# A two-block transformer kernel on one Trainium2 core: the mLSTM head norm spread over its neighbours, and weight halves and modulation slabs reordered at two norms

## The chip, the cores and the metric

The kernel runs on one core of a Trainium2 chip. The metric is the device time of one execution in microseconds. Three runs of the kernel before took 2473.16, 2465.38 and 2474.76 us; their median is 2473.16 us.

## The reference, cut to what matters

Two blocks are computed for 512 latent and 256 context tokens of width 1024, in fp32. The first ends in a convolutional feed-forward layer between two post-norms. The second starts with a mixer of two halves: an mLSTM (4 heads of 128, both directions over chunks of 128 tokens) and a banded window attention (8 heads of 64). What the change touches:

```python
def post_norm(x, y, gate, g, b):
    return layer_norm(ALPHA * x + gate * y) * g + b

def modulate(x, shift, scale):
    return layer_norm(x) * (1 + scale) + shift          # first block
    # second block: rms_norm(x, g) * (1 + scale) + shift

def mlstm_out(h, oa):                                    # h = forward + backward mLSTM output
    h = rms_norm(h.transpose(0, 2, 1, 3), a_norm_g.reshape(A_HEADS, A_HEAD_DIM))
    return (h.reshape(b, t, A_WIDTH) * sigmoid(oa)).astype(oa.dtype)

y = concatenate([mlstm_out(ha, oa), ob], axis=-1) @ w_out    # ob: the window attention
```

The shifts, scales and gates are six rows of `silu(c) @ w_ada + b` for each block.

## The kernel before, in words

The program is a row of blocks. In each block every engine (TensorE, VectorE, ScalarE, GpSimd, and SyncE for the transfers) has its own list of instructions in a fixed order, and the semaphores are written out by hand; all engines meet at a block's end. Activations lie with channels on the partitions (xT, hT: 8 tiles of 128 channels by 768 tokens), the latent range is 512 columns and the context range 256.

All big weights come as slabs of 1024 x 256 through a ring of four slots. `load_slabs` (L321) issues the load of a slab once the slab four places before has been used. A slab of a projection is split into two exact parts: ScalarE copies a half (128 columns) in rounded form (`high`, L1027 and L2538), GpSimd subtracts (`low`, L1033 and L2586), and TensorE makes three products per tile with the parts of the activations. A slab of the modulation (`ada_slab`, L852) is used straight from the ring by 8 matmuls; it gives its slot back when they are done.

Three places matter.

**The norms ahead of the feed-forward layer (ln1) and ahead of the second mixer (ln2).** At both, a post-norm (`post`) is followed by the modulated norm of the next stage (`norm`). A norm that centres sums its input over the 8 tiles on TensorE (L448), takes the mean on ScalarE (L556), spreads it over the partitions (L456), subtracts it on VectorE (L614), squares on ScalarE (L572), sums the squares (L448), takes the root (ScalarE L536) and the reciprocal (VectorE L605), spreads it (L456), multiplies (VectorE L630), and applies gain and shift on ScalarE (`outs`, L598). A split norm then writes the rounded part (VectorE L640) and the rest (GpSimd L646), tile by tile, and TensorE starts on the projection with the first tile. Two hooks let other work in: `gaps`, run by TensorE at named places, and `fill`, run by ScalarE right after the root. Before, at ln1, the four slabs of the gate modulation stand in the gaps "mean" and "root" of the two norms, and `post.fill` copies three weight halves: two of the first slab of `ffn_w_up`, and one of the second. At ln2, `norm` does not centre, and it is the kind that does its context range first (`ctx_first`): its latent squares are taken on ScalarE (L589) from what VectorE has just scaled, and its sums follow on TensorE after the spread of the context range. There all four modulation slabs stand in one gap, "start", between the post-norm's spread and the norm's, and `post.fill` copies three halves of the first two slabs of `ab_w_in` and the narrow part.

**The mLSTM recurrence (L3495 on).** 12 steps, forward and backward in turn. Per step: TensorE makes the gate rows (L3505), the scores (L3512), the outputs (L3528, L3529) and the state update (L3535); ScalarE takes two exponentials (L3611 "iw", L3613); GpSimd scales queries and keys (L3627, L3628); VectorE masks (L3548, L3556, L3559), takes the denominators (L3572 to L3575), and updates the state (L3590). The first direction to reach a chunk writes its output by ScalarE (L3603), the second adds to it by VectorE (L3580); that second kind is steps 2, 3, 8, 9, 10 and 11. ScalarE ends with four sigmoids (L3618).

**The head norm (L3639 to L3689)** is a block of its own: squares on ScalarE (L3643), their sums on VectorE (L3664), root (L3647), reciprocal (L3666), six multiplications on VectorE (L3668), 24 transposes on TensorE (L3688), and eight copies out with the norm's gain (L3654, L3675). It also turns the key halves of the attention (L3681, L3661).

**The attention's pairs (L3047 on).** 24 pairs of a pair of heads and a token chunk, numbered p. Per pair: scores on TensorE (L3091), masked maximum on VectorE (L3161), exponential on ScalarE (L3201), division on VectorE (L3171, L3173), transposes on TensorE (L3103) and copies out of them (ScalarE L3209, VectorE L3181), values on TensorE (L3117), and their copy out (L3215), which GpSimd splits (L689, L690). Pairs with n = 1, 2 are wide (5 key blocks), those with n = 4, 5 are short (2 blocks). At pairs 0 to 3 GpSimd also multiplies the mLSTM half by the sigmoids and splits it (`gated_side`: L3056, L689, L690 on 128 x 768). Twelve modulation slabs are used at the short pairs (L852). Before pair 0, GpSimd writes the mask bands (L3064 to L3066) and VectorE the negated sinks (L3146).

The order of one pair on TensorE is written out by hand:

```python
for p in range(n_p):
    if p + 2 < n_p:
        scores(p + 2)
    ...
    turn(p)
    if p >= 1:
        values(p - 1)
```

## Time and profile before

| | us |
|---|---|
| three runs | 2465.38, 2473.16, 2474.76 |
| median | 2473.16 |
| profiled execution, its own time | 2473.65 |
| its span, first to last instruction | 2471.8 |
| mean granted TensorE clock, share of full | 0.968 |

The profiled execution is one run of the same program with the hardware profiler on. Its own time is 1.85 us more than its span. Times in the rows count from the first instruction. PE is TensorE's matmuls, PEld its weight loads, DVE VectorE, ACT ScalarE, POOL GpSimd, SP the queue of transfers; "PEq" as a releaser is TensorE's sequencer, which stands here for the end of a block. A matmul's duration contains its run through the array, so the pace of a row of them is read from start to start.

### The profile page before, as it was taken

The page shows a single profiled execution, that of the slowest core. Times are in us where ns is not written, and L with a number is a line of the kernel's source. Part 1 is how long each engine was busy: PE and PEld are TensorE (multiplying, and loading weights), DVE is VectorE, ACT ScalarE, POOL GpSimd, SP SyncE. Part 2 cuts the span into 40 slices and gives each one's busy share as a digit, 9 for nine tenths or more (in the row PEclk, how much of TensorE's full clock was granted, in tenths as well). Part 3 has the DMA queues.
Part 4 walks back from the last instruction along what each step waited for, and adds up shares of the span by engine and source line. Part 5 has one row for each costly group of instructions (what it writes and reads, how often), then busy time and mean ns, then how long its engine had stood idle before and what let it go on. Part 6 is the DMA issues. An engine that isn't in the chain of part 4 may idle for free. (4 is left out here: it accounts for less than half of the span.)

```text
span 2471.8 us, 35014 instructions
## 1 busy us (share of the span) xinstructions
PE 2334.2 (94%) x14351; PEld 1921.0 (78%) x14351; DVE 1151.1 (47%) x1893; ACT 797.6 (32%) x1343; POOL 1052.1 (43%) x715
## 2 busy tenths in 40 slices
PE   6999979999997999969899999999999999999999
PEld 5876747878774789856778888888887788788887
DVE  4647368665635660678345151322347652411111
ACT  4334353333325312335242121111134364322221
POOL 3436345555544122323246343433443024746553
PEclk8999989999997999979999999999999999999999
DMA  8335235444452111005112132321212102223221
GB/s 265 105 102 171 86 103 187 158 140 146 151 166 82 39 52 60 27 1 188 52 35 85 53 103 93 96 95 59 69 43 69 35 1 69 85 87 118 88 86 47
DMA packets 223933, 228.39 MB, mean 92 GB/s; under 512 B 7375, under 2 KB 221347, under 8 KB 223779
## 3 DMA queue, kind: packets, MB, share of 16 engines
q1 hardware_dynamic: 223443, 226.09, 28.4%
q8 instruction: 114, 1.87, 0.3%
q14 instruction: 40, 0.33, 0.0%
q10 hardware_dynamic: 336, 0.11, 0.0%
HBM read 224.08 MB, written 2.10 MB: 92 GB/s over the span
## 5 line engine op out<-in xcount | busy, mean ns | idle before, releaser
L1411 POOL TENSOR_TENSOR w_lo<-ring,w_hi 128x1024 fp32r<-128x1024 f32 x124 | 301.2, 2432 | 315.7 <-ACT w_hi L1405 315.7
L2355 DVE SCALAR_TENSOR_TENSOR xT<-ps,mods,xT 128x512 f32<-128x512 f32 (+1 forms) x160 | 108.4, 683 | 546.3 <-PE ps L1473 510.1
L1405 ACT ACTIVATE w_hi<-ring 128x1024 fp32r<-128x1024 f32 x124 | 130.6, 1057 | 503.4 <-PE ps L1473 503.4
L1471 PE MATMUL ps<-hidden_hi,w_hi 128*128 128x512 f32 (+1 forms) x768 | 272.4, 355 | 0.0
L1472 PE MATMUL ps<-hidden_lo,w_hi 128*128 128x512 f32 (+1 forms) x768 | 272.1, 354 | 0.0
L1473 PE MATMUL ps<-hidden_hi,w_lo 128*128 128x512 f32 (+1 forms) x768 | 271.8, 354 | 0.0
L2644 DVE SCALAR_TENSOR_TENSOR ffn_sums<-ps,cols,ffn_sums 128x441 f32<-128x441 f32 (+2 forms) x352 | 214.9, 686 | 105.8 <-ACT ffn_sums L2563 105.8
L1471 PE MATMUL ps<-h_hi,w_hi 128*128 128x512 f32 (+1 forms) x720 | 255.6, 355 | 3.6 <-POOL w_lo L1411 2.1
L1472 PE MATMUL ps<-h_lo,w_hi 128*128 128x512 f32 (+1 forms) x720 | 255.2, 354 | 0.0
L1473 PE MATMUL ps<-h_hi,w_lo 128*128 128x512 f32 (+1 forms) x720 | 254.8, 354 | 0.0
L2586 POOL TENSOR_TENSOR ffn_w_lo<-ring,ffn_w_hi 128x1024 fp32r<-128x1024 f32 (+2 forms) x76 | 161.7, 2129 | 191.9 <-ACT ffn_w_hi L2538 191.9
L1054 PE MATMUL ps<-h_hi,w_halves 128*128 128x512 f32 (+1 forms) x560 | 205.7, 367 | 11.1 <-POOL ab_lo L646 5.2
L2724 DVE TENSOR_TENSOR squares<-squares 128x512 f32<-128x512 f32 (+1 forms) x72 | 96.5, 1341 | 217.9 <-ACT squares L2710 217.9
L1471 PEld LDWEIGHTS ps<-hidden_hi,w_hi 128*128 128x128 f32 x768 | 145.3, 189 | 21.1 <-issue 0.8
L1033 POOL TENSOR_TENSOR ring_low<-ring,w_halves 128x1024 fp32r<-128x1024 f32 x31 | 77.1, 2494 | 197.2 <-ACT w_halves L1027 197.2
L1473 PEld LDWEIGHTS ps<-hidden_hi,w_lo 128*128 128x128 f32 x768 | 145.2, 189 | 20.3
L1472 PEld LDWEIGHTS ps<-hidden_lo,w_hi 128*128 128x128 f32 x768 | 145.3, 189 | 19.8
L1471 PEld LDWEIGHTS ps<-h_hi,w_hi 128*128 128x128 f32 x720 | 136.2, 189 | 24.4 <-POOL w_lo L1411 2.8
L2538 ACT ACTIVATE ffn_w_hi<-ring 128x1024 fp32r<-128x1024 f32 (+2 forms) x76 | 71.9, 947 | 255.9 <-PE ps L2527 233.7
L1473 PEld LDWEIGHTS ps<-h_hi,w_lo 128*128 128x128 f32 x720 | 136.1, 189 | 19.0
L1472 PEld LDWEIGHTS ps<-h_lo,w_hi 128*128 128x128 f32 x720 | 136.2, 189 | 18.7
L1054 PE MATMUL ps<-h_hi,ring_low 128*128 128x512 f32 (+1 forms) x384 | 134.8, 351 | 0.0
(473 smaller groups left out, 5192.1 us busy)
## 6 DMA issues: line engine op xcount, KB each, us to landing
ring<-in_mlp_w SPq DMA_DIRECT2D x64, 1024.0 KB, 5.3
ring<-in_ada_w SPq DMA_DIRECT2D x48, 1024.0 KB, 5.3
ring<-in_w_ada SPq DMA_DIRECT2D x24, 1024.0 KB, 5.3
ring<-in_ffn_w_up SPq DMA_DIRECT2D x22, 1024.0 KB, 5.3
ring<-in_ab_w_in SPq DMA_DIRECT2D x11, 1024.0 KB, 5.3
ring<-in_ffn_w_down SPq DMA_DIRECT2D x12, 768.0 KB, 4.5
ring<-in_w_in SPq DMA_DIRECT2D x8, 1024.0 KB, 8.6
ring<-in_c_w_in SPq DMA_DIRECT2D x6, 1024.0 KB, 5.0
```

The costliest lines, as they stand in the source:

```text
L1033: pool.tensor_tensor(low_half(h), ring_half(h), w_halves[:, h % 3, :, :].bitcast(F32), ALU.subtract)\
L1054: ins = pe.matmul(o, stationary, moving, start=(k == 0 and i == 0), stop=(k == KT - 1 and i == 2))
L1405: act.activation(w_hi[m][:, 0:x["kt"], :], ring[:, x["n"] % NS, 0:x["kt"], m * P:(m + 1) * P], ACT.Copy).then_inc(SW["w_hi"].sem, 1)
L1411: pool.tensor_tensor(w_lo[m][:, 0:x["kt"], :], ring[:, x["n"] % NS, 0:x["kt"], m * P:(m + 1) * P], w_hi[m][:, 0:x["kt"], :].bitcast(F32), ...
L1471: pe.matmul(o, w_hi[m][:, k, :], h, start=(k == 0), stop=False)
L1472: pe.matmul(o, w_hi[m][:, k, :], l, start=False, stop=False)
L1473: ins = pe.matmul(o, w_lo[m][:, k, :], h, start=False, stop=(k == x["kt"] - 1))
L2355: return nc.vector.scalar_tensor_tensor(x, bank, column_of(gates, t * 2 + 2 * gate + r), x, ALU.mult, ALU.add)
L2538: act.activation(w_hi[i % NW][:, 0:kt, :], ring[:, n % NS, 0:kt, m * P:(m + 1) * P], ACT.Copy).then_inc(SW["w_hi"].sem, 1)
L2586: pool.tensor_tensor(w_lo[i % NW][:, 0:kt, :], ring[:, n % NS, 0:kt, m * P:(m + 1) * P], w_hi[i % NW][:, 0:kt, :].bitcast(F32), ALU.subtract)\
L2644: ins = dve.scalar_tensor_tensor(o, on_grid(ps[:, (first + m) % 4, :])[:, y0 + dy:y1 + dy, x0 + dx:x1 + dx], cols[:, CW + tap * 2 * FT + t ...
L2724: dve.tensor_tensor(sq, sq, sq, ALU.mult).then_inc(v_order.sem, 1)
```

## The change

The head norm's block is dissolved. Its squares and their sums are taken by ScalarE in the recurrence, one chunk at a time once both directions have added to it (steps 2, 3, 8, 9, 10), each as four squares of 128 x 128 with an accumulator; the last chunk's, the root and the reciprocal open the attention's block. GpSimd multiplies (six times 128 x 512) ahead of the pairs. TensorE's 24 transposes come in six lots behind pairs 3, 4, 5, 6, 9 and 10, through one bank, and ScalarE copies them out. The gating of the mLSTM half moves from pairs 0 to 3 to pairs 11 to 14. The turned key halves are made in step 0 of the recurrence, the bands and the sinks in the block of transposes before it. The state update is left out in the last two steps, where nothing reads it. The table for the root is loaded at the end of the recurrence.

At both norms the four modulation slabs now follow the second and the fifth sum of squares of `post` and of `norm`, and `post.fill` copies only the two halves of the first slab; the rest is copied in `norm.fill`.

```diff
@@ -493,6 +493,7 @@
             for k in range(KT):
                 self.wait(pe, "sq", KT + k + 1)
                 self.sig(self.sums(pe, 0, squares[:, k % 3, 0:LAT], 192, LAT // 4, k == 0, k == KT - 1), "sq_used")
+                self.in_gap(pe, k)
...
@@ -502,6 +503,8 @@
                 self.lead.pe(pe, u)
             self.wait(pe, "sq", u + 1)
             self.sig(self.sums(pe, r, squares[:, u % 3, 0:n], 192 + c, w_, k == 0, k == KT - 1), "sq_used")
+            if r == 0:
+                self.in_gap(pe, k)
...
@@ -588,6 +591,8 @@
                     self.next.wait(act, "sq_used", KT + k - 2)
                 self.next.sig(act.activation(squares[:, k % 3, 0:LAT], self.where(k), ACT.Square,
                                              bias=self.shift(k, 0), scale=self.scale(k, 0)), "sq")
+            if self.next.fill is not None:
+                self.next.fill(act)
             self.next.root(act, 0, 2 * KT)
...
-            def late_slabs(pe):
-                for j in range(4):
-                    ada_slab(pe, 1, W["ada_2"] + j, 0, j, j == 3)
+            def late_slab(j):
+                return lambda pe: ada_slab(pe, 1, W["ada_2"] + j, 0, j, j == 3)
...
-                norm.gaps = {"start": late_slabs}
+                post.gaps = {1: late_slab(0), 4: late_slab(1)}
+                norm.gaps = {1: late_slab(2), 4: late_slab(3)}
                 post.pe(pe)
...
-                for h in range(0 if post is not None else 1, min(3, n_halves)):
+                for h in range(2 if post is not None else 1, min(3, n_halves)):
...
+            def first_parts(act):
+                for h in range(2):
+                    high(act, h)
...
-                (norm if post is None else post).fill = rest_of_parts
+                else:
+                    post.fill = first_parts
+                norm.fill = rest_of_parts
...
-        post.gaps = {"mean": gate_slab(0), "root": gate_slab(1)}
-        norm.gaps = {"mean": gate_slab(2), "root": gate_slab(3)}
+        post.gaps = {1: gate_slab(0), 4: gate_slab(1)}
+        norm.gaps = {1: gate_slab(2), 4: gate_slab(3)}
...
+        def first_parts(some):
+            def fill(act):
+                for i in some:
+                    high(i)
+            return fill
+        post.fill, norm.fill = first_parts(range(2)), first_parts(range(2, NW))
...
+                mix.wait_out(pool, mix.needed(i))
                 g_order.step(pool, pool.tensor_tensor(dst, dst, factor, ALU.mult))
                 made.split(pool, i, 0, TOK)
...
-            g_order.step(pool, pool.memset(bands, 0.0))
-            pool.tensor_copy(bands[:, PREV * CH:(PREV + 1) * CH], mats[:, M_PREV, :])
-            sig(pool.tensor_copy(bands[:, NEXT * CH:(NEXT + 1) * CH], mats[:, M_NEXT, :]), "bands")
+            mix.scaled(pool)
             for p in range(n_p):
-                if p < len(side):
-                    gated_side(pool, p)
+                if p in mix.side_at:
+                    gated_side(pool, mix.side_at.index(p))
...
+                    mix.wait_out(pe, mix.turns_until(p))
                     pe.wait_ge(ADA["ada_rows_out"].sem, ADA["ada_rows_out"].at(p // 6))
                 turn(p)
                 if p >= 1:
                     values(p - 1)
+                if p in mix.turn_at:
+                    mix.turn(pe, mix.turn_at.index(p))
...
-            wait(dve, "bands", 1)
-            sig(dve.tensor_scalar(nsink, rows[:, SINK:SINK + B_HEADS], -1.0, None, ALU.mult), "nsink")
-            wait(dve, "nsink", 1)
...
             top(0)
+            mix.inverse(dve)
...
+            mix.roots(act)
             expo(0)
...
                     give(p - 1)
+                if p in mix.turn_at:
+                    mix.out(act, mix.turn_at.index(p))
...
+        dve.tensor_scalar(nsink, rows[:, SINK:SINK + B_HEADS], -1.0, None, ALU.mult)
         transpose_out(dve, groups, 0)
...
+        g_order.step(pool, pool.memset(bands, 0.0))
+        for at, mask in ((2, M_PREV), (4, M_NEXT)):
+            pool.tensor_copy(bands[:, at * CH:(at + 1) * CH], mats[:, mask, :])
...
+n_mem = n_m - 2
+def chunk_squares(act, c):
+    for h in range(4):
+        ins = act.activation(sq_junk[:, h * P:(h + 1) * P], h_tok[:, c, h, :], ACT.Square, accum_out=ssq[:, c, h:h + 1])
+    return ins
...
         front(0)
+        for r, (t0, n) in enumerate(BOTH):
+            ins = pe.matmul(ps[:, 6 + r, 0:n], mats[:, SWAP, :], kb[:, 0, t0:t0 + n], start=True, stop=True)
+        sig(ins, "swapped")
...
+            if s >= n_mem:
+                continue
             wait(pe, "kw", s + 1)
+            if s == 0:
+                wait(pe, "out_v", 1)
...
             if s + 1 < n_m:
                 masked(s + 1)
+            if s >= n_mem:
+                continue
...
+                wait(act, "h", s + 1)
+                chunk_squares(act, c)
...
+                wait(act, "swapped", 1)
+                for r, (t0, n) in enumerate(BOTH):
+                    ins = act.activation(kb[:, 1, t0:t0 + n], ps[:, 6 + r, 0:n], ACT.Copy)
+                sig(ins, "out_v")
             if s >= 1:
                 give(s - 1)
-        give(n_m - 1)
         for t in range(4):
             act.activation(oa[:, t, :], oa[:, t, :], ACT.Sigmoid)
+        act.activation(warm[:, :], eps_col, ACT.Sqrt)
...
-sq_tok = k_tok.rearrange("p c (h e) -> p c h e", h=4)
-ssq = small[:, 0:4 * NCH].rearrange("p (c h) -> p c h", h=4)
-R = named("sq", "ssq", "std", "scaled", "turned", "out_a", "out_v", "swapped")
-out_groups = [(h, c0, n) for h in range(4) for c0, n in ((0, NLAT), (NLAT, NCTX))]
-bank_of = lambda g: (out_groups[g][0], 0) if out_groups[g][1] == 0 else (4 + out_groups[g][0] % 2, 256 * (out_groups[g][0] // 2))
-with nc.Block() as block:
-    @block.scalar
-    def _(act):
-        for j in range(3):
-            sig(act.activation(sq_tok[:, 2 * j:2 * j + 2, :, :].rearrange("p c h e -> p (c h e)"),
-                               h_tok[:, 2 * j:2 * j + 2, :, :].rearrange("p c h e -> p (c h e)"), ACT.Square), "sq")
-        wait(act, "ssq", 3)
...
-        a_order.step(act, act.activation(flat_s, flat_s, ACT.Sqrt, bias=eps_col, scale=1.0 / P))
-        sig(act.activation(flat_s, flat_s, ACT.Copy), "std")
...
-    @block.vector
-    def _(dve):
-        wait(dve, "swapped", 1)
-        for r, (t0, n) in enumerate(BOTH):
-            dve.tensor_copy(kb[:, 1, t0:t0 + n], ps[:, 6 + r, 0:n])
-        for j in range(3):
-            wait(dve, "sq", j + 1)
-            sig(dve.tensor_reduce(ssq[:, 2 * j:2 * j + 2, :], sq_tok[:, 2 * j:2 * j + 2, :, :], AX_X, ALU.add), "ssq")
-        wait(dve, "std", 1)
...
-    @block.tensor
-    def _(pe):
-        for r, (t0, n) in enumerate(BOTH):
-            ins = pe.matmul(ps[:, 6 + r, 0:n], mats[:, SWAP, :], kb[:, 0, t0:t0 + n], start=True, stop=True)
-        sig(ins, "swapped")
-        for c in range(NCH):
-            wait(pe, "scaled", c + 1)
-            for h in range(4):
-                b, o = bank_of(2 * h + int(c >= NLAT))
-                o += (c - (NLAT if c >= NLAT else 0)) * CH
-                ins = pe.transpose(ps[:, b, o:o + CH], h_tok[:, c, h, :], ident)
-        sig(ins, "turned")
-for n, v in (("sq", 3), ("ssq", 3), ("std", 1), ("scaled", NCH), ("turned", 1), ("out_a", 4), ("out_v", 4), ("swapped", 1)):
...
+class MixerNorm:
+    turn_at, side_at = [3, 4, 5, 6, 9, 10], [11, 12, 13, 14]
+    units = [[(h, c) for c in range(NLAT)] for h in range(4)] + \
+            [[(h, NLAT + c) for h in (2 * j, 2 * j + 1) for c in range(NCTX)] for j in range(2)]
+    BANK = 7
+    def __init__(self):
+        self.R = named("ssq", "std", "rd", "scaled", "swapped", "out_a")
+        self.flat = ssq.rearrange("p c h -> p (c h)")
+        self.src = qa.rearrange("p t n -> p (t n)").rearrange("p (c h e) -> p c h e", c=NCH, h=4)
...
+    def needed(self, i):
+        return 5 + i // 2
+    def turns_until(self, p):
+        return sum(at < p for at in self.turn_at)
+    def roots(self, act):
+        self.sig(chunk_squares(act, order_m[-1][1]), "ssq")
+        self.wait(act, "ssq", 1)
+        self.sig(act.activation(self.flat, self.flat, ACT.Sqrt, bias=eps_col, scale=1.0 / P), "std")
+    def inverse(self, dve):
+        self.wait(dve, "std", 1)
+        self.sig(dve.reciprocal(self.flat, self.flat), "rd")
+    def scaled(self, pool):
+        self.wait(pool, "rd", 1)
         for c in range(NCH):
-            sig(dve.tensor_tensor(h_tok[:, c, :, :], h_tok[:, c, :, :],
-                                  ssq[:, c, :].unsqueeze(2).to_broadcast([P, 4, P]), ALU.mult), "scaled")
...
+            self.sig(pool.tensor_tensor(self.src[:, c, :, :], h_tok[:, c, :, :],
+                                        ssq[:, c, :].unsqueeze(2).to_broadcast([P, 4, P]), ALU.mult), "scaled")
+    def turn(self, pe, i):
+        self.wait(pe, "scaled", NCH)
+        if i:
+            self.wait(pe, "out_a", i)
+        for j, (h, c) in enumerate(self.units[i]):
+            ins = pe.transpose(ps[:, self.BANK, j * CH:(j + 1) * CH], self.src[:, c, h, :], ident)
+        self.sig(ins, "swapped")
+    def out(self, act, i):
+        self.wait(act, "swapped", i + 1)
+        runs = [(h, 0, NLAT, 0) for h in [i]] if i < 4 else \
+               [(h, NLAT, NCTX, (h % 2) * CTX) for h in (2 * (i - 4), 2 * (i - 4) + 1)]
+        for h, c0, n, o in runs:
+            ins = act.activation(hT[:, h, c0 * CH:(c0 + n) * CH], ps[:, self.BANK, o:o + n * CH], ACT.Copy,
+                                 scale=cols[:, COL["mlstm_norm"] + h:COL["mlstm_norm"] + h + 1])
+        self.sig(ins, "out_a")
```

## Rows read from the trace of the kernel before

**Rows 1.** The page's first part: busy time of each engine

```profile
PE 2334.2 (94%) x14351; PEld 1921.0 (78%) x14351; DVE 1151.1 (47%) x1893; ACT 797.6 (32%) x1343; POOL 1052.1 (43%) x715
```

**Rows 2.** Windows of the attention: stretch, length, busy by engine, PEclk, DMA share, GB/s

```profile
1093.90:1107.00 13.10, 11.06 (x37) 5.74 (x38) 6.61 (x21) 4.83 (x13) 1.15 (x1) 0.50 0.00 0
1107.00:1199.00 92.00, 85.26 (x865) 57.15 (x864) 72.27 (x218) 48.59 (x136) 36.77 (x59) 0.96 0.43 138
```

**Rows 3.** Timeline, recurrence's end to first pairs: start, duration, engine, instructions, [idle before <-releaser]

```profile
1063.37 1.13 DVE L3580 SCALAR_TENSOR_TENSOR hT<-ps,small,hT 128x128 f32<-128x128 f32 x4
...
1063.37 1.28 ACT L3618 ACT_TABLE_LOAD   x1
1064.66 3.04 ACT L3618 ACTIVATE big<-big 128x768 f32<-128x768 f32 x4
1072.53 2.95 ACT L3643 ACTIVATE big<-hT 128x1024 f32<-128x1024 f32 x3 [4.82 <-PEq L3495]
...
1089.12 1.20 PE L3091 MATMUL ps<-big 64*128 64x256 f32 x8 [2.55 <-PEq L3639]
1093.94 2.94 PE L3091 MATMUL ps<-big 64*128 64x384 f32 x12 [3.62 <-DVE small L3161]
...
1092.33 0.15 DVE L3160 COPY big<-small 128x1 f32<-128x1 f32 x1
```

**Rows 4.** Timeline of two recurrence steps: ScalarE and VectorE

```profile
1025.90 0.60 ACT L3611 ACTIVATE hT<-ps 128x512 f32<-128x512 f32 x1 [1.65 <-PE ps L3505]
...
1048.51 1.14 ACT L3603 ACTIVATE hT<-ps,small 128x128 f32<-128x128 f32 x4 [0.47 <-DVE small L3575]
...
1024.72 1.13 DVE L3580 SCALAR_TENSOR_TENSOR hT<-ps,small,hT 128x128 f32<-128x128 f32 x4
1028.12 1.12 DVE L3548 TENSOR_SCALAR hT<-ps,small 128x128 f32<-128x128 f32 x4
```

**Rows 5.** Timeline of the attention's pairs (L3628: the recurrence): TensorE, VectorE, GpSimd

```profile
1118.55 0.66 PE L3103 MATMUL ps<-mats,big 128*128 128x128 f32 x4
...
1124.62 1.85 DVE L3173 TENSOR_SCALAR big<-big,small 128x512 f32<-128x512 f32 x1
1134.83 0.49 DVE L3173 TENSOR_SCALAR big<-big,small 128x512 f32<-128x512 f32 x1
...
1047.12 1.04 POOL L3628 TENSOR_TENSOR big<-big,small 128x512 f32<-128x512 f32 x1
...
1124.31 1.87 POOL L690 TENSOR_TENSOR h_hi<-hT,ab_out_hi 128x768 fp32r<-128x768 f32 x1
```

**Rows 6.** Timeline of the norms ahead of the feed-forward layer (ln1)

```profile
326.30 1.06 ACT L2538 ACTIVATE ffn_w_hi<-ring 128x1024 fp32r<-128x1024 f32 x1 [5.35 <-DMA ring<-in_ffn_w_up]
327.26 5.74 ACT L598 ACTIVATE xT<-xT,cols 128x512 f32<-128x512 f32 x8
...
328.12 5.59 PE L448 MATMUL ps<-xT,mats 128*32 128x128 f32 x64 [6.86 <-ACT xT L598]
336.11 1.94 PE L852 MATMUL ps<-ring,sil 128*32 128x256 f32 x16
```

**Rows 7.** Timeline of the norms ahead of the second mixer (ln2)

```profile
759.01 2.00 ACT L1027 ACTIVATE w_halves<-ring 128x1024 fp32r<-128x1024 f32 x2 [10.68 <-DMA ring<-in_ab_w_in]
...
751.48 4.87 DVE L630 TENSOR_TENSOR xT<-xT,ps 128x512 f32<-128x512 f32 x8 [2.17 <-PE ps L456]
...
751.37 5.69 PE L852 MATMUL ps<-ring,sil 128*32 128x256 f32 x64
764.11 1.97 PE L456 MATMUL ps<-rstd,mats 128*128 128x64 f32 x8 [7.04 <-DVE rstd L605]
766.01 5.12 PE L448 MATMUL ps<-squares,mats 128*32 128x128 f32 x64
...
753.43 46.54 SPq L321 DMA_DIRECT2D ring<-in_ab_w_in  x5
```

**Rows 8.** Window within ln1: columns as in the second group

```profile
328.00:339.00 11.00, 10.14 (x108) 4.75 (x112) 2.78 (x5) 7.34 (x13) 1.81 (x1) 0.50 0.00 0
```

52 lines of the change are left out of this document (24 added, 28 removed).

## The prediction

> **What bounds the kernel now.** I read the page first: TensorE is busy 94% of the span [rows 1], so almost everywhere only the matmuls set the time, and a change can gain only where TensorE stands still. Then the windows and the timelines of the three stages that the change touches, engine by engine, and the waits in them.
>
> Head norm. TensorE is nearly always busy in the recurrence and in the pairs (85.26 of 92 us there [rows 2]), but between them lies a serial block: from 1072.53 squares, sums, root, reciprocal, scaling, transposes and copies follow one another, and the attention's first scores start at 1089.12. The second scores start only at 1093.94, because they wait for VectorE's first maxima, and these wait for bands and sinks written at the block's start [rows 3].
>
> ln1. ScalarE stands 5.35 us before the third weight half until its slab lands, and behind it stands L598; TensorE waits 6.86 us for L598's first tile and then follows it tile by tile for 5.59 us [rows 6]. The clock granted there is 0.50, the lower of its two levels (1.2 GHz) [rows 8].
>
> ln2. TensorE runs all four slabs after the post-norm's spread; the first projection slab can only then be issued (753.43), and ScalarE waits 10.68 us for it in `post.fill` [rows 7]. Behind that stand the context's root, its spread (764.11), and the latent sums (766.01 to 771.13), on which the rest of the norm hangs.
>
> **The sum, part by part.** It is made against the profiled execution's own 2473.65 us (span 2471.8 and 1.85 around it), which is 0.5 above the median of the runs shown.
>
> A1, the block goes. VectorE's addition of step 10 ends at 1064.50 [rows 3]. ScalarE then has four squares with accumulators. No row shows a square of that shape. Below: four copies of 128 x 128 take 1.14 us in L3603 [rows 4]. Above: four pieces of 0.60, the time of a whole 512-column exponential, 2.4 us. I take 1.75, nearer the copies, with a little for each accumulator's read. Then the sigmoids' table and the sigmoids as now (1.28 and 3.04), and the root's table, priced as the other, 1.28 with 0.2 for its dummy root: 1064.5 + 1.75 + 4.33 + 1.5 = 1072.1. VectorE's last addition ends before that, its last state update (about 1.1 us) being gone. The meeting of the engines costs about 0.3, so with A2's 0.6 the attention's block opens at 1073.0. First scores 1.20, first maxima 1093.94 - 1092.33 = 1.6 [rows 3], and the second scores start at about 1075.9 instead of 1093.94: **-18.0**. Beside this, ScalarE takes the last chunk's squares (1.75), root (0.3) and the exponential's table (1.28), ready at 1076.4, hidden by the first scores and maxima but for half a us, which the next exponential absorbs; the reciprocal stands behind the first maxima on VectorE. GpSimd's six multiplications, at 1.04 each as L3628 [rows 5], end near 1082.5, long before TensorE wants them behind pair 3.
>
> A2, squares in the recurrence. After steps 2, 3, 8 and 9 they stand on ScalarE ahead of the next step's first exponential. VectorE's addition ends at 1025.85, it wants that exponential's result at 1028.12, and the exponential takes 0.60 [rows 4]: 1.67 us are free, and 1.75 are needed. Behind the delayed exponential GpSimd's query scaling waits, which TensorE wants 3 us later. Four steps by 0.1 to 0.2: **+0.6**, counted above; 0 to 3 by the ends of the square's price. The turning of the keys in step 0 (two matmuls, two copies of some 1.0 us) meets a TensorE that waits for VectorE anyway: 0, at most 0.5. The bands and sinks move to a block whose copies outlast them: 0.
>
> A3, what TensorE gets back in the pairs. Twenty-four transposes in six lots of four; four take 0.66 with the tail, about 0.59 from start to start [rows 5]: 6 x 0.59 = **+3.5**, on the path, since TensorE is the bound there. ScalarE's copies (4.3 us in all) lie in its idle time, and the one bank is free again a pair later. Ends: +3 and +6, if the lots also make it wait.
>
> A4, GpSimd's gating later. Four times L3056, L689, L690, some 4.5 us each by L690's 1.87 [rows 5] and its neighbours, now at pairs 11 to 14, three of which have no modulation slab to lengthen TensorE's part. What the row shows: L3173 takes 0.49 alone and 1.85 while GpSimd runs [rows 5]. At pairs 0 to 3 this cost TensorE nothing visible, so 0 is the lower end; above, half of GpSimd's 18 us beyond VectorE's slack, some 5 us. I take **+1.5**, near the row. The queue of transfers is not moved past anything here. A in all: -18.0 + 3.5 + 1.5 = **-13.0**; -16 to -7.
>
> The Trainium skill, page "GPSIMD Engine Reference", section "Specifications", says that GpSimd shares its SBUF interfaces with VectorE and contends with instructions in a two-port mode or with two SBUF inputs. By that rule every L3173 beside the moved work is held, and the trace agrees (1.85 against 0.49).
>
> B1, ln1. The first gate slab now ends behind the second sum of squares, near 315.9, 2.3 us later than now; its successor's load needs about 5 us, so ScalarE gets its halves at 321.0, copies two (2.0) and starts L598 at 323.0 instead of 327.26: **-4.3**. The third half is copied after the next root, in idle time. The price: two slabs now stand between the norm's sums instead of in gaps with free time. At full clock they fit between squares that come every 0.6 us: 0.3. At half clock each takes 1.94 [rows 6] and the sums run late by up to 3.4. The wait before L598's first tile shrinks from 6.9 us to about 2.5, so the clock may stay up. I take +1.8, the middle, as the rows show no wait of 2.5 here: B1 = **-2.5**; -5.5 (full clock, a faster spread too) to +0.5.
>
> B2, ln2. The first slab ends near 745.2; issue to use took 5.6 us (753.43 to 759.01), so the halves are copied from 750.9 to 752.9. The context's root follows, but its reciprocal stands on VectorE behind L630, which ends at 756.35 [rows 7]: that is what is late next. Reciprocal to 757.0, spread 1.97, sums 5.12 [rows 7] and two slabs of 1.94: 768.0 at half clock, against 771.1 now, -3.1. All at full clock, with the fill ahead of the root: 763.5, -7.6. Before, the clock granted rose while the four slabs ran densely; here the dense work begins only at 757, so I take half of the stretch as fast: B2 = **-4.5**, ends -8 and -1. Loads of later slabs are issued some 9 us later, 20 us before they are needed.
>
> Sum: 2473.65 - 13.0 - 2.5 - 4.5 = **2453.6 us**, 0.8% below before.
>
> **The rivals.** First, only the head norm pays: the slabs between the sums run at half clock and eat what the earlier L598 and halves give. For: 0.50 in both stretches [rows 8]. Against: at ln2 even half clock leaves 3 us. 2473.65 - 13 + 0 = 2460.6.
>
> Second, the clock stays up: shorter waits keep TensorE at 2.4 GHz through both norms. -5.5 - 8 - 15 gives 2445. For: through the post-norms, with matmuls for a third of the time, it was full. Against: it was low behind each of these long waits [rows 8].
>
> Third, VectorE becomes the pairs' bound: the 18 us of gating hold L3173 wherever they meet it. With nearly all of them on the path (+13) A is about -3, and with B 2463. For: [rows 5]; against: pairs 1 to 4 bore the same work and TensorE hardly idled.
>
> Fourth, slower. The removed block held 24 transposes in a row; without them the clock, low from the recurrence's end until 1107 now [rows 2], rises later. Pairs at half clock take twice TensorE's time; each us of full-clock work so done costs one. From 20 us of such work, five pairs, the gain is gone; with eight pairs, some 30 us, it is 2484. Against: scores two onward keep TensorE dense, as before.
>
> That the change doesn't do what it says I give nothing: each hook has its caller in the diff.
>
> **How the numbers follow.** Forecast 0.6, only the head norm 0.15, clock up 0.12, VectorE 0.09, slower 0.04. A measurement of this kernel tells about 0.5%, 12 us, from no change, i.e. 2461. The forecast's own bounds, not all at once, give 2445 to 2461; to this come the rivals on either side and the runs' own 4 us: 2442 to 2464 leaves out the slow case and the fastest part of the second. Faster by over 0.5%: the forecast, the clock case and the first rival, 0.87, less 0.03 for the runs' scatter about the last, which lies near the bound: 0.84. Within: 0.12. Slower: 0.04.
>
> **What would show it.** Right: second scores of the attention about 18 us earlier against the recurrence's start; TensorE gapless through pairs 3 to 10 and longer by 3.5; L598 in ln1 starting with two halves and no third ahead of it; in ln2 the reciprocal of the context right behind L630, and the latent root 3 to 5 us earlier. Wrong: L3611 late by over 0.5 us per step, TensorE idle at pairs 11 to 14, PEclk of 0.5 past the attention's second pair, or ScalarE waiting for a slab in either norm for longer than 3 us.

## The result and the profile after

The changed kernel takes 2440.64 us (median of 4 runs, 2438.72 to 2442.74), the kernel before in the same measurement 2471.5 (2465.38 to 2474.76): ratio 0.9881, 95% interval 0.9865 to 0.9896. Measured once more beside 17 runs of before (e6, below) the ratio is 0.9905, interval 0.9890 to 0.9920. So it is faster by some 1 to 1.2%, 23 to 29 us, where 20 were forecast. The sign and the kind were right; 2440.64 itself lies 1.4 below the range's lower end.

Lines of the norms stand 5 lower in the changed kernel (L598 is L603, L852 is L857), scores L3091 are L3103, the scaling L3173 is L3184.

First part of the page of the changed kernel [rows 1], then two windows of it, its columns as in [rows 2]: the first pairs and the rest of them.

```profile
PE 2314.1 (95%) x14335; PEld 1909.8 (78%) x14335; DVE 1143.0 (47%) x1870; ACT 805.5 (33%) x1394; POOL 1060.4 (43%) x719
```

```profile
1062.78:1074.90 12.12, 10.12 (x34) 5.45 (x36) 6.77 (x21) 5.39 (x13) 6.21 (x6) 0.50 0.00 0
1074.90:1171.00 96.10, 87.88 (x894) 58.64 (x890) 73.64 (x220) 53.43 (x146) 41.68 (x62) 0.98 0.41 132
```

The stretch at half clock behind the second scores has stayed (12.1 us against 13.1), so the slower rival is out. TensorE's work per pair has grown.

To see where the time went I took the starts of the same TensorE instructions in each trace and cut the span there. Differences of starts, in us; the last two columns are all the rest of the span, and the span. The cuts, with their starts before and after: the context's last transposes ahead of ln1 (308.03, 306.70), a product at the end of the feed-forward layer (735.96, 732.20), the first product of the second mixer's projection (779.86, 769.35), the recurrence's first step (1007.66, 995.70), the attention's second scores (1093.94, 1062.78), the tiles of L861 (1189.31, 1162.65), the first product of the output projection (1199.18, 1171.11).

| profile | ln1 and feed-forward | ln2 | recurrence to second scores | pairs to L861 | their end | the rest | span |
|---|---|---|---|---|---|---|---|
| before | 427.94 | 43.89 | 86.28 | 95.37 | 9.87 | 1808.5 | 2471.8 |
| before again (e5) | 428.13 | 43.73 | 86.55 | 95.31 | 9.75 | 1808.1 | 2471.6 |
| after | 425.50 | 37.15 | 67.08 | 99.87 | 8.46 | 1800.8 | 2438.8 |
| after again (e6) | 425.54 | 37.15 | 67.08 | 99.87 | 8.45 | 1801.4 | 2439.5 |
| e1, head norm only | 428.13 | 43.76 | 67.09 | 101.02 | 9.82 | 1804.8 | 2454.6 |
| e2, ln1 only | 425.60 | 43.44 | 84.26 | 95.13 | 9.65 | 1805.1 | 2463.2 |
| e3, ln2 only | 428.00 | 37.14 | 86.54 | 95.16 | 9.80 | 1807.2 | 2463.8 |
| e4, weights early | 425.76 | 37.15 | 67.07 | 99.73 | 6.86 | 1801.7 | 2438.2 |
| e7, without ln1 | 427.56 | 37.18 | 68.02 | 100.78 | 9.69 | 1805.9 | 2449.1 |
| e8, without ln2 | 425.68 | 41.56 | 67.09 | 99.88 | 10.12 | 1804.0 | 2448.3 |
| e9, few transposes | 425.63 | 37.15 | 67.09 | 97.90 | 9.70 | 1809.7 | 2447.1 |
| e10, gating in slab pairs | 425.77 | 37.15 | 67.07 | 99.89 | 8.46 | 1800.8 | 2439.1 |
| e11, squares twice | 425.65 | 37.14 | 72.54 | 100.24 | 9.29 | 1803.1 | 2448.0 |
| e12, gating and weights | 425.62 | 37.15 | 67.22 | 97.16 | 6.85 | 1805.0 | 2439.0 |

Between the first profiles the edited stages give -2.4, -6.7, -19.2, +4.5 and -1.4, in all -25.3. The rest of the span gives another 7.7, without an edit in it. Over the fourteen profiles that rest is anything from 1800.8 to 1809.7, and I can tie its value to no edit (the changed kernel, 1800.8, and e9, 1809.7, do the same work there). Part of it may be low clock, of which the whole span has less after (by the mean clock, 0.968 before and 0.976 after, (1 - 0.968) x 2471.8 / 0.5 = 158 us before against 117). The mean clock alone doesn't give it either: e9 and e11 have the same, 0.972, and rests of 1809.7 and 1803.1. A single pair of profiles is thus no measure of the total. A stage is a better one, but not an exact one: where e2 has the old mixer its recurrence to second scores lasts 84.26 and not 86.3 to 86.5, where e8 has the old ln2 that lasts 41.56 and not 43.4 to 43.9, and the same pairs take 99.87 in the change and 101.02 in e1.

**The opening.** Timeline of the changed kernel, from the last recurrence step to the second pair [rows 3]:

```profile
1053.87 1.28 ACT L3663 ACT_TABLE_LOAD   x1
1055.16 3.04 ACT L3663 ACTIVATE big<-big 128x768 f32<-128x768 f32 x4
1057.98 1.13 DVE L3617 SCALAR_TENSOR_TENSOR hT<-ps,small,hT 128x128 f32<-128x128 f32 x4
1058.21 1.28 ACT L3664 ACT_TABLE_LOAD   x1
1060.00 1.14 PE L3103 MATMUL ps<-big 64*128 64x256 f32 x8 [2.66 <-PEq L3525]
1062.64 0.30 DVE L3718 RECIPROCAL small<-small 128x24 f32<-128x24 f32 x1
1062.78 2.94 PE L3103 MATMUL ps<-big 64*128 64x384 f32 x12 [1.64 <-DVE small L3172]
1063.02 6.21 POOL L3723 TENSOR_TENSOR big<-hT,small 128x512 f32<-128x512 f32 x6 [12.52 <-DVE small L3718]
```

The serial block of squares, sums, root, scaling and transposes is gone. The first scores come 2.0 behind the start of the last addition, the reciprocal stands on VectorE behind the first maxima and holds nothing back, and GpSimd scales beside the pairs. What sets the opening now is ScalarE's row of sigmoids and two tables.

**The squares in a step** (timeline of a recurrence step, ScalarE and VectorE, [rows 4]):

```profile
1042.19 0.31 ACT L3521 ACTIVATE squares<-hT 128x128 f32<-128x128 f32 x1 [1.63 <-DVE hT L3617]
...
1043.28 0.19 ACT L3521 ACTIVATION_READ_ACCUMULATOR squares<-hT 128x1 f32 x1
1043.37 0.57 ACT L3652 ACTIVATE hT<-ps 128x512 f32<-128x512 f32 x1
...
1044.43 1.12 DVE L3585 TENSOR_SCALAR hT<-ps,small 128x128 f32<-128x128 f32 x4
```

Four squares with their reads take 1.28 (1042.19 to 1043.47), and VectorE takes the exponential's result 0.5 behind its end. All steps keep their length: against before, the first step's values start 11.95 earlier and the last step's 11.94.

**The pairs** (timeline of the changed kernel, [rows 5]): a lot of transposes between the values ahead of it and the scores behind it; an instruction of GpSimd's first gating with the VectorE scaling beside it, and TensorE's three waits; the third gating, which begins just before a modulation slab on TensorE; and the two subtractions of the next weights at pair 19 with the longest wait.

```profile
1083.74 1.31 PE L3129 MATMUL ps<-big 128*64 128x128 f32 x20
1084.98 0.66 PE L3731 MATMUL ps<-mats,big 128*128 128x128 f32 x4
1085.57 1.13 PE L3103 MATMUL ps<-big 64*128 64x256 f32 x8
...
1123.04 1.81 POOL L695 TENSOR_TENSOR h_hi<-hT,ab_out_hi 128x768 fp32r<-128x768 f32 x1
1123.23 1.96 DVE L3184 TENSOR_SCALAR big<-big,small 128x640 f32<-128x640 f32 x1
1125.45 0.74 PE L3115 MATMUL ps<-mats,big 128*128 128x128 f32 x5 [0.51 <-DVE big L3184]
1126.60 0.73 PE L3115 MATMUL ps<-mats,big 128*128 128x128 f32 x5 [0.41 <-DVE big L3192]
1130.36 0.74 PE L3115 MATMUL ps<-mats,big 128*128 128x128 f32 x5 [0.67 <-DVE big L3192]
1131.95 2.00 POOL L3070 TENSOR_TENSOR hT<-hT,big 128x768 f32<-128x768 f32 x1
1132.90 1.07 PE L857 MATMUL ps<-ring,sil 128*32 128x256 f32 x16
...
1157.13 4.71 POOL L689 TENSOR_TENSOR ab_out_w<-ring,ab_out_w 128x1024 fp32r<-128x1024 f32 x2
1157.89 1.76 DVE L3184 TENSOR_SCALAR big<-big,small 128x256 f32<-128x256 f32 x1
1159.76 2.24 DVE L3184 TENSOR_SCALAR big<-big,small 128x256 f32<-128x256 f32 x1
1162.65 1.92 PE L866 MATMUL ps<-mats,mean 128*128 128x32 f32 x12 [3.65 <-DVE big L3192]
```

**ln1** (timeline, [rows 6]): the first gate slab now runs behind the second sum, the load behind it is issued at 314.65, and two halves, not three, stand ahead of L603.

```profile
313.54 1.05 PE L857 MATMUL ps<-ring,sil 128*32 128x256 f32 x16
314.65 2.16 SPq L321 DMA_DIRECT2D ring<-in_ffn_w_up  x2
319.75 2.00 ACT L2549 ACTIVATE ffn_w_hi<-ring 128x1024 fp32r<-128x1024 f32 x2 [2.00 <-DMA ring<-in_ffn_w_up]
321.65 5.74 ACT L603 ACTIVATE xT<-xT,cols 128x512 f32<-128x512 f32 x8
322.51 5.59 PE L448 MATMUL ps<-xT,mats 128*32 128x128 f32 x64 [2.57 <-ACT xT L603]
333.04 1.93 PE L857 MATMUL ps<-ring,sil 128*32 128x256 f32 x16
```

**ln2** (timeline, [rows 7]), and two windows of it with the granted clock (0.50, then 1.00):

```profile
741.52 47.92 SPq L321 DMA_DIRECT2D ring<-in_ab_w_in  x5
746.74 2.00 ACT L1032 ACTIVATE w_halves<-ring 128x1024 fp32r<-128x1024 f32 x2 [2.18 <-DMA ring<-in_ab_w_in]
746.79 4.87 DVE L635 TENSOR_TENSOR xT<-xT,ps 128x512 f32<-128x512 f32 x8 [1.25 <-PE ps L456]
751.58 0.54 DVE L610 RECIPROCAL rstd<-rstd 128x64 f32<-128x64 f32 x1
...
760.70 0.35 ACT L539 ACTIVATE rstd<-ps,mats 128x128 f32<-128x128 f32 x1
```

```profile
747.20:757.40 10.20, 5.22 (x56) 4.08 (x60) 4.92 (x9) 5.37 (x8) 4.67 (x2) 0.50 0.19 60
757.50:764.20 6.70, 3.45 (x61) 2.07 (x52) 1.87 (x3) 6.70 (x11) 2.76 (x2) 1.00 0.97 305
```

ScalarE's 10.68 us for the slab are 2.18 now, and the context's reciprocal starts in the moment in which VectorE's last product L635 ends, as forecast.

### The profile page after: what moved, and what is told of

Same layout as the page of the kernel before. It is cut to its first block and busy times, and to the rows that moved or that the text cites. A ratio compares the mean times of both kernels' runs of the same rounds, so it can differ in the third digit from the quotient of the medians.

```text
span 2438.8 us, 35010 instructions
## 1 busy us (share of the span) xinstructions
PE 2314.1 (95%) x14335; PEld 1909.8 (78%) x14335; DVE 1143.0 (47%) x1870; ACT 805.5 (33%) x1394; POOL 1060.4 (43%) x719
## 5 line engine op out<-in xcount | busy, mean ns | idle before, releaser
L2549 ACT ACTIVATE ffn_w_hi<-ring 128x1024 fp32r<-128x1024 f32 (+2 forms) x76 | 71.9, 947 | 252.5 <-PE ps L2538 234.3
```

The costliest lines, as they stand in the source:

```text
L2549: act.activation(w_hi[i % NW][:, 0:kt, :], ring[:, n % NS, 0:kt, m * P:(m + 1) * P], ACT.Copy).then_inc(SW["w_hi"].sem, 1)
```

## The experiments

My theory was that the three parts add up, each worth what its own stage shows. The rival was that they help each other through the clock. First each part alone, then the change without one part, with both kernels beside them.

**e1, the head norm alone.** The kernel before with the change's hunks from L2995 on (the mixer's), none of those in the norms.

> The kernel before with the mixer's part of the change alone (squares in the recurrence, scaling, transposes and gating in the pairs); both norms as before. Theory: the parts add up, each worth what its own stage shows between the two traces. From the recurrence's first step to the first product of the projection behind the attention that is 1007.66 to 1199.18 = 191.5 before and 995.70 to 1171.11 = 175.4 after: 16.1 less, and up to 1.9 more where the clock is granted full behind it; so about 2471.5 - 17 = 2454.5, ratio 0.993. The second scores start 67.1 behind the recurrence's first step (86.3 before). Rival: the three parts help each other, through the clock that each leaves to what follows; then this part alone gives less, 10 or so (2461), though its own stage is shorter by the same 16, and the rest is spread over stages without an edit.

Measured: 2452.82 against 2465.34, ratio 0.9941 (0.9924 to 0.9957), 14.6 us by the ratio; the two medians alone differ by 12.5. The gains of e2 and e3 below are by the ratio too. TensorE's timeline of e1:

```profile
1007.31 1.13 PE L3522 MATMUL ps<-mats,small 128*128 128x128 f32 x8 [0.83 <-PEq L3460]
...
1074.40 2.95 PE L3090 MATMUL ps<-big 64*128 64x384 f32 x12 [1.65 <-DVE small L3159]
```

67.09 from step 0 to the second scores, as in the whole change, and 19.2 less than before. The pairs last 101.02, 1.2 more than in the whole change; the clock behind the opening stays low 3 us longer there. From the recurrence to the projection e1 is 13.6 shorter than before (177.93 against 191.52), which fits its total.

**e2, ln1 alone.**

```diff
-                post.gaps = {"mean": gate_slab(0), "root": gate_slab(1)}
-                norm.gaps = {"mean": gate_slab(2), "root": gate_slab(3)}
+                post.gaps = {1: gate_slab(0), 4: gate_slab(1)}
+                norm.gaps = {1: gate_slab(2), 4: gate_slab(3)}
...
+                post.fill, norm.fill = first_parts(range(2)), first_parts(range(2, NW))
```

> The kernel before with the slabs and weight halves reordered ahead of the feed-forward layer alone. Theory: 2.4 less (shift of the two traces from -1.33 at the stage's start to -3.72 at its end), 2469, ratio 0.999; L598's first tile starts some 4.3 earlier against the start of the sums, and the norm's own sums, with two slabs between them at half clock, give 2 of it back. Rival: stages without an edit gain as well, 4 or more in all.

Measured: 2464.94 against 2465.34, ratio 0.9994 (0.9983 to 1.0005). The stage is 2.3 shorter in the trace (427.94 to 425.60); the total can't show it.

**e3, ln2 alone.**

```diff
-                        norm.gaps = {"start": late_slabs}
+                        post.gaps = {1: late_slab(0), 4: late_slab(1)}
+                        norm.gaps = {1: late_slab(2), 4: late_slab(3)}
...
+                            post.fill = first_parts
+                        norm.fill = rest_of_parts
```

> The kernel before with the slabs and weight halves reordered ahead of the second mixer alone. Theory: 6.5 less in its own stage, 2465, ratio 0.9974: the first projection slab is issued some 8 us earlier against the sums, the halves are ready before VectorE's last product of the post-norm, and the context's reciprocal stands right behind that product. Rival: with ln1 as before, less, about 4.

Measured: 2463.51, ratio 0.9980 (0.9969 to 0.9992), 4.9 us. Its stage lasts 37.14, in the whole change 37.15, some 6.7 less than in the first profile of before. The rival's 4 is out for this profile; e8 below shows that the old order doesn't always take as long as it did there.

**e5, before again**, no edit.

> The kernel before, unchanged, for a second profile. Its executions gather near 2465 and near 2473; the profile shown is of 2473.65. Theory: the two groups differ only in how many 3.4 us stretches of low clock fall into stages that no edit touches (the stages before ln1, the projections, the last mixer); a profile near 2465 has 10 to 15 us less of them and the same times in ln1, ln2 and the recurrence as the first. Rival: an execution near 2465 has a shorter ln1 or ln2 of its own, so the parts of the change gain less against it than the stages showed.

Measured: 2468.22 (2462.82 to 2474.27), ratio 0.9993 to the other runs of before. Its profiled execution took 2473.34, near the first, and so told nothing of a run near 2465: why the runs of before scatter by over 10 us stays open. The stages of the two profiles agree within 0.3. But e2's profile, of an execution that took 2465.05 with the old mixer, has the recurrence to the second scores at 84.26, with a mean granted clock of 0.91 there against 0.88 before. e3's profile, of 2465.61, has 86.54. So the theory's same times hold in one of these two profiles and not in the other.

**e6, after again**, no edit.

> The changed kernel, unchanged, on the chip and in the rounds of the others. Both theories: 2440.6, ratio 0.988 to 0.990. By the sum of the three parts run alone (ratios 0.9941, 0.9994 and 0.9980, that is 14.6, 1.5 and 4.9) it should be 2465.3 - 21 = 2444.3; the rest, if it stays, is what the parts do for each other.

Measured: 2445.11 (2441.32 to 2446.6), ratio 0.9905 (0.9890 to 0.9920). 2469.75 - 2445.11 is 24.6, by the ratio 23.5. The parts alone sum to 21.0. Their intervals together are wider than the 2.5 between: nothing is left that the parts must do for each other, and a few us that they might do are not ruled out either.

**e7, after without ln1**, and **e8, after without ln2**: the diffs of e2 and e3 taken back.

> The changed kernel with the slabs and halves ahead of the feed-forward layer put back. Theory, parts add up: 2440.6 + 2 = 2442.6 (its stage alone lasts 2.4 longer). Rival, the parts help each other through the clock: what ln1 gives depends on what follows, and it costs 5 or more, 2446.

> The changed kernel with the slabs and halves ahead of the second mixer put back. Theory, parts add up: 2440.6 + 6.5 = 2447. Rival: more, 10 or so, since the projections behind it then have low clock again.

Measured: e7 2446.66, ratio 0.9909 (0.9892 to 0.9926), 1.5 above e6; e8 2450.35, ratio 0.9927 (0.9913 to 0.9942), 5.2 above e6. Both agree with the parts alone: 1.5 and 5.2 with the other parts in, 1.5 and 4.9 alone. For e8 the rival's 10 is out. For e7 the interval is 8 us wide and can't tell the theory's 2 from the rival's 5; what speaks for 2 is its stage, 427.56 against 425.50. The old ln2 in e8 lasts 41.56, 4.4 more than the new one, where it was 6.7 between the first profiles; its mean granted clock is 0.76 there, and was 0.72 before. ScalarE's timelines of e7 and of e8 have the old waits back:

```profile
325.81 1.06 ACT L2549 ACTIVATE ffn_w_hi<-ring 128x1024 fp32r<-128x1024 f32 x1 [4.13 <-DMA ring<-in_ffn_w_up]
```

```profile
755.65 2.00 ACT L1032 ACTIVATE w_halves<-ring 128x1024 fp32r<-128x1024 f32 x2 [8.34 <-DMA ring<-in_ab_w_in]
```

**e9, the price of the transposes.**

```diff
-                for j, (h, c) in enumerate(self.units[i]):
+                for j, (h, c) in enumerate(self.units[i][:1]):
```

> The changed kernel with one transpose in place of four in each of the six lots; 18 of 24 are left out, so three quarters of the normalised heads don't reach the projection. Theory: the transposes are paid in full on TensorE, 18 x 0.147 = 2.6: the pairs from the fourth to the wait ahead of L866 last 77.08 - 2.6 = 74.4. Rival: the pairs are held by VectorE and GpSimd; then they keep 76 or more, and the transposes were free.

Measured: pairs 97.90 against 99.87, so the 18 transposes left out cost 1.97, 0.11 each. That is the price of the second to the fourth of a lot. The one that stays takes 0.25 up to the next scores (1085.80 to 1086.05), the lot of four 0.59 (1084.98 to 1085.57), and six times the difference is 2.0. So 24 transposes don't cost 24 times 0.11: the values ahead of a lot take the same 1.24 to the next start with a lot behind them (1083.74 to 1084.98) as without one (1079.84 to 1081.08), the whole lot is added, and six lots cost the 3.5 that were forecast. The first of the six lots lies ahead of the fourth pair's cut, which is why I take the whole of the pairs; the stretch named in the expectation went from 77.08 to 75.42. They are on TensorE's path, so the rival, that they were free, is out. The total, 2449.27 (ratio 0.9926), is above that of the change: its rest is 1809.7, the longest of all profiles. It can't be used for 2 us.

**e10, the gating moved.**

```diff
-            turn_at, side_at = [3, 4, 5, 6, 9, 10], [11, 12, 13, 14]
+            turn_at, side_at = [3, 4, 5, 6, 9, 10], [11, 12, 15, 16]
```

> The changed kernel with the gatings of pairs 13 and 14 moved to pairs 15 and 16, which have a modulation slab on TensorE. Theory: the three waits of TensorE for VectorE at pairs 13 and 14 (0.51, 0.41 and 0.67) go, and none comes at 15 and 16: 77.08 - 1.6 = 75.5 for the pairs. Rival: the wait follows the gating; 77.1.

Measured: 2445.13, ratio 0.9906 (0.9890 to 0.9923), pairs 99.89. A miss for my theory. Timeline of GpSimd in e10:

```profile
1119.67 1.82 POOL L3070 TENSOR_TENSOR hT<-hT,big 128x768 f32<-128x768 f32 x1
1125.57 1.82 POOL L3070 TENSOR_TENSOR hT<-hT,big 128x768 f32<-128x768 f32 x1
1136.85 1.83 POOL L3070 TENSOR_TENSOR hT<-hT,big 128x768 f32<-128x768 f32 x1
1142.19 1.82 POOL L3070 TENSOR_TENSOR hT<-hT,big 128x768 f32<-128x768 f32 x1
```

TensorE's three waits are still there (0.51, 0.41 and 0.67, the last at 1129.80). They belong to the first two gatings, which I had left where they were; I had taken them for the third and fourth. GpSimd comes to a gating late: the one numbered 11 starts at 1120.24 in the changed kernel and runs into TensorE's pair 13, and the next into pair 14, the two of the four without a modulation slab. The third and fourth met pairs with a slab at either place and cost nothing. So e10 moved the wrong two. Its theory, that a slab hides a gating, fits the changed kernel's own trace but wasn't tested.

**e11, the squares twice.**

```diff
-                        chunk_squares(act, c)
+                        a_order.step(act, chunk_squares(act, c))
+                        chunk_squares(act, c)
```

> The changed kernel with each chunk's four squares in the recurrence taken twice, one after the other (1.28 to 1.3 more on ScalarE behind steps 2, 3, 8, 9 and 10, nothing left out). In the changed kernel the squares end just as TensorE's columns come, and the exponential behind them starts at once. Theory: ScalarE has no slack left there but VectorE has about 0.5 before it wants the exponential, so each of four steps grows by 0.7 to 1.0 and the last by 1.3: the recurrence up to the first scores lasts 64.31 + 4.6 = 69 (68 to 70). Rival: ScalarE has slack in the recurrence as in the pairs; 1.3 more at the end alone, 65.6.

Measured: 2449.92, ratio 0.9932 (0.9913 to 0.9952); recurrence up to the first scores 68.83 against 64.31, +4.5 where 4.6 were expected. VectorE's timeline of e11 shows the wait for the late exponential and the new step, 5.96 in place of 5.20:

```profile
1048.59 1.13 DVE L3585 TENSOR_SCALAR hT<-ps,small 128x128 f32<-128x128 f32 x4 [0.84 <-issue]
1054.55 1.13 DVE L3585 TENSOR_SCALAR hT<-ps,small 128x128 f32<-128x128 f32 x4 [0.84 <-issue]
```

So one set of squares fits and a second does not: 1.3 more on ScalarE (with the order kept between the sets) makes a step 0.76 longer, so there is room for about half a us behind the first set.

**e4, weights early**, a try at the 3.65 us wait that both kernels have at the end of the pairs.

```diff
-                        if p == 19:
+                        if p == 16:
                             made.weights_high(act)
...
-                        if p == 19:
+                        if p == 17:
                             made.weights_low(pool)
```

> The changed kernel with the halves of the output projection's first weights taken earlier: copies on ScalarE at pair 16 in place of 19, subtractions on GpSimd at pair 17 in place of 19. At pair 19 GpSimd's two subtractions (4.7 us) hold VectorE's scaling at 1.76 and 2.24 in place of 0.49, and TensorE stands 3.65 us behind it, before and after alike. Theory: at pairs 15 to 18 TensorE has a slab's work in each pair, so the same hold is hidden there and the wait goes: 3 to 3.6 less than the changed kernel, 2437, ratio 0.986 against before. Rival: VectorE has no more slack there than at 19, and the wait moves with the work: 2440.6 as after; or worse, if the slab has not landed when ScalarE asks for it.

Measured: 2440.16, ratio 0.9889 (0.9871 to 0.9907). Timelines of VectorE, GpSimd and TensorE in e4:

```profile
1149.25 4.92 POOL L689 TENSOR_TENSOR ab_out_w<-ring,ab_out_w 128x1024 fp32r<-128x1024 f32 x2
1152.06 2.45 DVE L3184 TENSOR_SCALAR big<-big,small 128x640 f32<-128x640 f32 x1
1155.39 0.74 PE L3115 MATMUL ps<-mats,big 128*128 128x128 f32 x5 [2.44 <-DVE big L3192]
```

The scaling that meets the second subtraction is held for 2.45. The wait moved with the work and lost a third. The pairs with their end are 1.7 shorter (106.59 against 108.33), and all but 0.1 of it lies behind L866, where the clock stays up. The total is where the rival had it.

**e12, the gating of e10 and the weights in eight pieces.**

```diff
-                            made.weights_low(pool)
+                            made.weights_piece(pool, p - 17)
...
+            def weights_piece(self, pool, step):
+                m = step // 2
...
+                for q in range(2):
+                    k = 4 * (step % 2) + 2 * q
+                    ins = pool.tensor_tensor(self.w_lo[m][:, k:k + 2, :], ring[:, self.n % NS, k:k + 2, m * P:(m + 1) * P],
+                                             self.w_hi[m][:, k:k + 2, :].bitcast(F32), ALU.subtract)
```

> e10 and, besides, the weights' halves of e4 in eight pieces of 128 x 256 (0.6 each), two behind each of pairs 17 to 20, in place of two subtractions of 2.4 in a row. In e4 the wait of TensorE only moved (2.44 at pair 18 in place of 3.65 at 21), since the two in a row held both of VectorE's scalings to their ends. Theory: a hold is as long as the GpSimd instruction that it meets; pieces of 0.6 hold by no more than that, and the pairs hide it: 3.6 + 1.6 less than the changed kernel, pairs to L866 71.9, and with less waiting the clock stays up behind them. 2440 - 5 = 2435, ratio 0.986 to 0.988. Rival: the sum of the holds is what counts, in pieces as in whole: 2438 to 2440.

Measured: 2438.53 (2437.43 to 2440.78), ratio 0.9881 (0.9862 to 0.9899). In the same rounds e10, which differs by the weights alone, took 2445.13: 6.6 less, though the two intervals of the ratio overlap by a little. Its pairs with their end last 104.01 against 108.35 in e10. Timelines of GpSimd, VectorE and TensorE in e12:

```profile
1153.31 1.42 POOL L698 TENSOR_TENSOR ab_out_w<-ring,ab_out_w 128x256 fp32r<-128x256 f32 x2
1157.57 0.70 DVE L3195 TENSOR_SCALAR big<-big,small 128x512 f32<-128x512 f32 x1
1160.97 0.63 DVE L3195 TENSOR_SCALAR big<-big,small 128x256 f32<-128x256 f32 x1
1162.25 1.53 PE L877 MATMUL ps<-mats,mean 128*128 128x32 f32 x12 [0.57 <-DVE big L3203]
```

Beside the pieces no scaling takes longer than 0.70, and the wait of 3.65 is 0.57. The pairs from the fourth to L877 take 73.33; the forecast 71.9 counted on the 1.6 that e10 didn't give. The pieces are not only smaller than e4's subtractions, they are also spread over four pairs; which of the two took the wait away no run separates. By its own stage e12 is the fastest version, 4.3 below the change's 108.33. By the total that isn't shown: its ratio is the one that the change had in the first measurement, and 2438.53 is in the rival's range.

## Why the prediction was right or wrong

**A1, the opening: right, short by 1.2.** Forecast -18.0, shown -19.2 in e1 and in the whole change. The term that was off is the price of the squares, 1.75 "nearer the copies, with a little for each accumulator's read": they take 1.28 with the reads and end 1.31 behind the addition, 0.4 less than the forecast has. Another 0.6 is A2, and the little that is left I don't assign. The -19.2 is against a stage of 86.3; against e2's 84.26, with more of the removed block at full clock, the same opening is worth 17.2. A gain from a block that stands largely at half clock depends on the clock that it happened to get, and the forecast had no term for that.

**A2, squares in the recurrence: forecast +0.6, shown 0.** The free time of 1.67 was read rightly; it is the same price that failed, 1.28 in place of the 1.75 needed, which leaves 0.4 (the trace has 0.5 between the exponential's end and VectorE's next start). That such room is small was right (e11).

**A3, transposes: forecast +3.5, right.** Each lot of four adds 0.59 from start to start, and TensorE has no gap of over 0.1 from the fourth pair to the first gating.

**A4, the gating: forecast +1.5, shown about +1.3** (waits of 1.59 against 0.31 before in that part), by the mechanism forecast: L3184 at 1.96 beside GpSimd. The prediction says that three of the pairs 11 to 14 have no modulation slab; there are two, 13 and 14, since the slabs run at pairs 3 to 6, 9 to 12 and 15 to 18, and the waits stand at just these two. The pairs grew by 4.5 in all; 3.5 and 1.3 are 0.3 more than that, and the stretch at half clock is 1.0 shorter. The profile fits a stricter rule than the one I used: the Trainium skill, page "SBUF — State Buffer", section "SBUF: two separate sides", says that the port pair shared by GpSimd and VectorE is an exclusive lock, held for a whole instruction by whichever starts first, where the VectorE instruction is in a two-port mode or has two inputs in SBUF; that L3184 is in such a mode no trace here names. By that rule a scaling that comes second ends just behind the GpSimd instruction that it meets; the traces agree: 1123.23 + 1.96 = 1125.19 against 1124.85, and 1162.00 against 1161.84 for the second subtraction. In e12, where the second work is in pieces of a quarter of the size, the holds beside it end at 0.70; the gating, which is as before, still holds a scaling for 1.97.

**B1, ln1: right.** Forecast -2.5, shown -2.4. L603 starts at 321.65 in a trace that is 1.3 ahead when the stage begins, so at 322.98 on the old scale, forecast 323.0. The price was paid as forecast too: a slab among the norm's own sums takes 1.93, at half clock, and of some 4.3 gained 2 go back.

**B2, ln2: the mechanism right, forecast -4.5, shown -6.7 between the profiles, 4.4 in e8.** On the old scale (3.8 ahead at the stage's start) the context's reciprocal starts at 755.3 instead of ending at 757.0, since VectorE's product starts at 750.5 there and at 751.48 before: the spread ahead of it (745.60) runs ahead of the low clock, which begins at 747.2. Then the sums with two slabs were priced half at low clock; in the trace the clock is full from 757.5, and the latent root comes at 764.5 on the old scale, where 766.6 was implied. "Half of the stretch" was the estimate that failed. The root is 6.7 earlier than before (771.20), not the 3 to 5 named as a sign. And what the old order costs depends on its clock: with 0.76 in e8 the new one gains 4.4, near the forecast.

**The end of the pairs** gives -1.4 that no step had: behind the same wait of 3.65 there are some 3 us of low clock less. It isn't the change's by any mechanism that I can show; in e1, with the same edit, the end lasts 9.82 as before.

**The sum.** The steps forecast -20.0 (-13.0, -2.5, -4.5); the edited stages show -23.9 without the end (-14.7, -2.4, -6.7, each rounded). That agrees with the second measurement (-23.5). The first one's -29.4 lies beyond the sum by 5.5, about what the untouched rest of the span scatters by. The range started at 2473.65 and allowed 4 for the runs' scatter; that rest alone ranges over 9. So 2440.64 lies below the range for two reasons: the steps gave 4 us more than forecast, and the rest of the span came out short in this measurement, which was luck and no part of the argument.

**The rivals.** Only the head norm pays: out, e3 and e8. The clock stays up: partly true in ln2 alone. Its support, matmuls "for a third of the time" in the post-norms, isn't what the trace of before has: TensorE is busy for 7.37 of the 10 us from 311 to 321. VectorE as the pairs' bound: out, 1.3 of the 13. Its own sum was wrong, too: -18.0 + 3.5 + 13 is -1.5 and not -3, so the case stood at 2465, just outside the range. Slower through a late clock: out, 12.1 us at low clock against 13.1. It took the clock for low from the recurrence's end until 1107; the rows show that only from 1093.90 on, and the removed block had 0.59 on the mean. Of the signs named as wrong, one came: TensorE idle at the gatings, by 1.6.

## What to carry to other kernels

A serial block between two stages dissolves well when each of its pieces has an engine with proven idle time beside it. Price a piece on the engine that bounds the stage from start to start between its neighbours: here that gave 0.59 a lot and came out. Leaving out a part of a group gives the price of that part alone, as e9 did, and the first of a group costs more than the next. A load that gates a later stage is worth pulling ahead by moving the work that frees its buffer into waits that are already there, even at half clock. A long GpSimd instruction holds a VectorE scaling beside it to its own end; here cutting one into pieces and spreading them over four pairs took a wait of 3.65 down to 0.57. Where an engine runs behind the bounding one, look in the trace for the pair that its work really meets before moving it.

## What was not expected of the hardware

A square of 128 x 128 with its accumulator's read takes ScalarE 0.30 from start to start (0.31 and 0.19 overlap), hardly above a plain copy (1.14 for four).

Stages that no edit touches, some 1800 us, differ by up to 9 us between profiles, in part by stretches of some 3.4 us at half clock in dense matmuls. In the untouched products between 880 and 1007 such a stretch is there in eight of the fourteen profiles and costs 1.5 each time. All five profiles with the old ln1 have it and three of the nine with the new one; whether that is a relation or chance these profiles don't tell.
